# Four moves inside the attention stage of a two-block transformer kernel: VectorE's LRU product, GpSimd's sums and weight requests, and two PSUM reads

## The reference, cut to what matters

```python
def masked_softmax(s, mask):
    s = jnp.where(mask, s.astype(jnp.float32), NEG)
    return jax.nn.softmax(s, axis=-1) * mask
# nsa_mixer: per block of 128 queries, 8 heads, three branches
    p_cmp = masked_softmax(s, dist >= 0)            # over 31 compressed keys
    p = masked_softmax(s, (dist >= 0)[:, :, None])  # selected keys
    p = masked_softmax(s, mask)                     # window keys
    return (g * o).sum(axis=2).reshape(B, S, NSA_WIDTH)
# first_block
    y_a = (y_a * jax.nn.silu(g_nsa)) @ w_proj_a
    y_b = rglru_mixer(u_lru, conv_w, conv_b, lru_wa, lru_ba, lru_wx, lru_bx, lru_lambda)
    y_b = (y_b * jax.nn.silu(g_lru)) @ w_proj_b
    gate_a, gate_b = jnp.split(merge_g, N_BRANCHES, axis=-1)
    m = jax.nn.sigmoid(gate_a) * y_a + jax.nn.sigmoid(gate_b) * y_b
    x = x + m @ w_out
# second_block
    mod = (c @ w_ada[l] + b_ada[l])[:, None, :]
    shift1, scale1, gate1, shift2, scale2, gate2 = jnp.split(mod, 6, axis=-1)
```

## Time and profile before

| what | us |
|---|---|
| median of 3 runs | 1329.16 (1327.74 to 1331.72) |
| the profiled execution, its own time | 1331.02 |
| its span in the trace | 1329.2 |
| PE matmuls busy | 1220.5 (92%) |
| DVE busy | 584.6 (44%) |
| ACT busy | 302.9 (23%) |
| POOL busy | 261.6 (20%) |
| DMA of POOL's queue (q0) | 17.96 MB in 10176 packets |

### The profile page before, as it was taken

One profiled execution on the slowest core, in us unless ns is written; L12 is line 12 of the kernel. 1 busy time (PEld: TensorE's weight loads), 2 busy tenths in 40 slices (PEclk: granted clock), 3 DMA queues, 4 the chain that ended last, 5 costly groups with the idle time before them and its releaser, 6 DMA issues.

```text
span 1329.2 us, 13605 instructions
## 1 busy us (share of the span) xinstructions
PE 1220.5 (92%) x5048; PEld 712.3 (54%) x5048; DVE 584.6 (44%) x1469; ACT 302.9 (23%) x716; POOL 261.6 (20%) x218
## 2 busy tenths in 40 slices
PE   7899998899989999999999899999999799887785
PEld 3455446566744444588874446677654444333232
DVE  3114395588737751208972367422223522321121
ACT  3213643333310000223032255200001211110010
POOL 7200024355400000071600020313200112111100
PEclk9999998899999999999999999999999889988888
DMA  9525110214377612313140202202276589999992
GB/s 326 109 72 127 64 52 12 96 64 143 99 248 255 218 63 101 130 45 127 65 167 23 64 0 65 69 0 64 64 276 266 193 340 402 407 409 402 408 356 83
DMA packets 93255, 215.13 MB, mean 162 GB/s; under 512 B 20297, under 2 KB 51289, under 8 KB 81367
## 3 DMA queue, kind: packets, MB, share of 16 engines
q1 hardware_dynamic: 79664, 193.08, 39.6%
q0 software_dynamic: 10176, 17.96, 5.5%
q10 hardware_dynamic: 3344, 3.16, 0.7%
HBM read 207.79 MB, written 14.75 MB: 167 GB/s over the span
## 4 chain that ended last, share of the span: by engine, by line
PE 69%; SPq 12%; DVE 8%; DMA 5%; ACT 2%; issue 2%; POOL 0%; POOLq 0%; DVEq 0%; ACTq 0%
SPq L2849 11%; PE PS L2363 7%; PE PS L1038 5%; PE PS L1492 4%; PE PS L1570 4%; PE PS L2426 4%; PE PS L1754 4%; PE PS L1756 4%; PE PS L2532 3%; PE PS L612 3%; PE PS L2964 3%; PE PS L1800 2%; PE PS L1501 2%; PE PS L1812 2%; PE PS L682 2%
## 5 line engine op out<-in xcount | busy, mean ns | idle before, releaser
L1332 POOL TENSOR_SCALAR AN<-AN,SM 128x128 f32<-128x128 f32 (+3 forms) x64 | 78.6, 1236 | 198.9 <-DVE SM L1428 198.9
L2964 PE MATMUL PS<-AN,HT 128*64 128x512 f32 x272 | 87.3, 660 | 18.4 <-DMA AN<-in_w_up 8.7
L1355 DVE SCALAR_TENSOR_TENSOR AN<-AN,COLA 128x256 f32<-128x256 f32 x168 | 84.1, 501 | 5.0
L3043 DVE TENSOR_TENSOR HT<-HT,PS 128x256 f32<-128x256 f32 x16 | 6.7, 421 | 152.2 <-ACT HT L3021 152.2
L612 PE MATMUL PS<-W,HT 128*128 128x512 f32 (+1 forms) x192 | 70.5, 528 | 0.0
L2964 PEld LDWEIGHTS PS<-AN,HT 128*64 128x64 f32 x272 | 28.7, 153 | 73.6 <-issue 73.2
L1492 PE MATMUL PS<-HT,W 128*128 128x512 f32 x128 | 58.1, 599 | 0.0
L2532 PE MATMUL PS<-W,AN 128*128 128x512 f32 x128 | 57.6, 597 | 0.0
L1314 ACT ACTIVATE AN<-PS,SM 128x128 f32<-128x128 f32 (+3 forms) x64 | 33.7, 527 | 104.3 <-DVE SM L1405 104.0
L1570 PE MATMUL PS<-W,AN 128*128 128x512 f32 x128 | 55.5, 593 | 1.9 <-DVE GBC L1369 1.9
L2341 POOL TENSOR_TENSOR AN<-W 128x512 f32<-128x512 f32 x8 | 10.1, 1268 | 234.1 <-DMA W<-in_w_in 98.6
(11 more groups left out here) (530 smaller groups left out, 2351.7 us busy)
## 6 DMA issues: line engine op xcount, KB each, us to landing
W<-in_w_in SPq DMA_DIRECT2D x14, 2048.0 KB, 8.9
W<-in_w_down SPq DMA_DIRECT2D x20, 1024.0 KB, 23.0
AN<-in_w_ada SPq DMA_DIRECT2D x17, 1024.0 KB, 5.3
AN<-in_w_gate SPq DMA_DIRECT2D x15, 1024.0 KB, 18.4
AN<-in_w_up SPq DMA_DIRECT2D x15, 1024.0 KB, 29.2
AN<-in_w_down SPq DMA_DIRECT2D x12, 1024.0 KB, 18.9
W<-in_w_gate SPq DMA_DIRECT2D x10, 1024.0 KB, 21.7
W<-in_w_up SPq DMA_DIRECT2D x10, 1024.0 KB, 30.8
```

The source lines that it names most:

```text
L1332: pool.tensor_scalar(PU[u % 5][:, 0:n], PU[u % 5][:, 0:n], RSUM[:, u:u + 1], None, ALU.mult).then_inc(*sc_pool.up(u))
L1355: dve.scalar_tensor_tensor(out=a, in0=wt[:, c, :], scalar=ca["c2"][:, c:c + 1], in1=a, op0=ALU.mult, op1=ALU.add).then_inc(*ada_dve.up(p, c))
L2964: t = pe.matmul(u.ap[r, :].rearrange("p (n f) -> p n f", n=2), XGT[e % 2][:, c, r], w_gu(3 * e + half)[:, c], start=c == 0, stop=c == 7)
```

## The change

Nothing is added or removed; every engine executes the same instructions as before. Four things move.

1. DVE's product with GL (L1232, four instructions) goes from step 33 to step 34.
2. In `pool_attention` the request of a half part of `w_ada` stood ahead of the step's multiply L1332 and now stands behind it. The requests are now L1331 and the multiply L1327.
3. `dve_out` (L1434) goes from the end of its step to the start; `dve_mod` (L1373) goes from the start of the step with r == 3 to behind the scale in the step before.
4. GpSimd's sums of hT go behind two sets of small requests, of `cmp_b` (L773) and of the LRU's weights (L674).

```diff
         if step == 33:
->       if step == 34:
             wd.wait_ge(*lru_act.at("gl"))
             for m in range(4):
                 dve.tensor_tensor(UC[:, m, :], UC[:, m, :], GL[:, m, :], ALU.mult)...
 # pool_attention
         for step in range(NU + 2):
-            p, half = divmod(step - 34, 4)
-            if 0 <= p < ATT_PARTS and half in (0, 2):
-                wg.wait_ge(*(ada_dve.at(p - 1, 3 + 2 * half) if p else lru_dve.at("y", 3)))
-                pool.dma_start(STAGE[0]...).then_inc(*part_in[half // 2].up(p))
             u = step - 2
             if u >= 0:
                 n = (UNITS[u][0] + 1) * 128
                 wg.wait_ge(*sc_dve.at(u // 2, "gate"))
                 wg.wait_ge(*B.use("qk", u).out)
                 pool.tensor_scalar(PU[u % 5][:, 0:n], PU[u % 5][:, 0:n], RSUM[:, u:u + 1], ...)
+            p, half = divmod(step - 34, 4)
+            if 0 <= p < ATT_PARTS and half in (0, 2):
+                wg.wait_ge(*(ada_dve.at(p - 1, 3 + 2 * half) if p else lru_dve.at("y", 3)))
+                pool.dma_start(STAGE[0]...).then_inc(*part_in[half // 2].up(p))
 # dve_attention
             p, r = ada_at(step)
+            if step >= 22 and (step - 22) % 16 == 0:
+                dve_out(dve, wd, (step - 22) // 16)
             if step in FILL and fill_at(step)[2] and fill_at(step)[1] != 1:
                 dve_group(dve, wd, *fill_at(step)[:2])
-            if r == 3 and 0 < p <= ATT_PARTS:
-                dve_mod(dve, wd, p - 1)
 ...
             if step >= 2 and step % 2 == 0 and step <= NU:
                 dve_scale(dve, wd, step // 2 - 1)
+            if r == 2 and 0 < p <= ATT_PARTS:
+                dve_mod(dve, wd, p - 1)
             if step in SUM_AT:
                 dve_group_sum(dve, wd, *SUM_AT[step])
-            if step >= 22 and (step - 22) % 16 == 0:
-                dve_out(dve, wd, (step - 22) // 16)
 # pool_program
-        pool_sums(pool, wg)
         pool_b1(pool, wg)
         pool_bd(pool, wg)
+        pool_sums(pool, wg)
```

More of the change, by code:

```diff
@@ L1228, in dve_lru @@
             dve.tensor_tensor_scan(UC[:, m, :], RG[:, m, :], IG1[:, m, :], 0.0, ALU.mult, ALU.add).then_inc(*lru_dve.up("h", m))
-        if step == 33:
+        if step == 34:
             wd.wait_ge(*lru_act.at("gl"))
@@ L1321, in pool_attention @@
         for step in range(NU + 2):
-            p, half = divmod(step - 34, 4)
-            if 0 <= p < ATT_PARTS and half in (0, 2):
-                wg.wait_ge(*(ada_dve.at(p - 1, 3 + 2 * half) if p else lru_dve.at("y", 3)))
-                pool.dma_start(STAGE[0].rearrange("p (c n) -> p c n", c=8)[:, 2 * half:2 * half + 4],
-                               wada[:, 2 * half:2 * half + 4, 256 * PARTS[p]:256 * PARTS[p] + 256]).then_inc(*part_in[half // 2].up(p))
             u = step - 2
@@ L1332, in pool_attention @@
                 pool.tensor_scalar(PU[u % 5][:, 0:n], PU[u % 5][:, 0:n], RSUM[:, u:u + 1], None, ALU.mult).then_inc(*sc_pool.up(u))
+            p, half = divmod(step - 34, 4)
+            if 0 <= p < ATT_PARTS and half in (0, 2):
+                wg.wait_ge(*(ada_dve.at(p - 1, 3 + 2 * half) if p else lru_dve.at("y", 3)))
+                pool.dma_start(STAGE[0].rearrange("p (c n) -> p c n", c=8)[:, 2 * half:2 * half + 4],
+                               wada[:, 2 * half:2 * half + 4, 256 * PARTS[p]:256 * PARTS[p] + 256]).then_inc(*part_in[half // 2].up(p))
     def ada_sum(p):
```

## The result

The changed kernel takes 1362.09 us in the median of four runs (1357.38 to 1365.89), beside 1330.44 us for the kernel before: a ratio of 1.0238, with a 95% interval of 1.0199 to 1.0277. It is slower by 31.7 us. The forecast was 1344.3 us, with a range up to 1353: the direction was right, and the forecast of 15.1 us slower was about half of what it is. The profiled execution has a span of 1363.7 us and took 1365.89; PE is busy for 1230.9 us of it (90%), before for 1220.5 us with the same 5048 matmuls.

What follows compares the result with a forecast made beforehand. PE, busy 92% of the span, was taken as the bound. The loop's 14.7 us less 1.1 of slack, 13.6, plus 1.5 for the clock gave +15.1: median 1344.3 us, range 1340 to 1350, 8 in 10 within 1335 to 1353.

Steps and rivals of the forecast that it cites:

- The loop: Steps 34 to 62: scale, multiply, request, landing, use, scale form 14 links, together 118.0 us against 101.5 before.
- the landing, 4.0 us for all 14: Each w_ada half-part request in the loop takes 4.0 us from issue to landing, the median in the kernel before.
- rival of longer landings: Landings of 4.5 us in the mean cost 7 us more, half speed at both places 3.2: 1354.5 us; chance 0.08.
- The start of the loop: The scale of step 34 ends at 256.5 us in place of 258.3, 1.8 us earlier.
- The product's gain: PE's wait for L1249 falls from 5.5 to 2.4 us and the half-speed stretch goes: 5.5 us on PE, alone.
- The clock's price: Steps 38/39 and 54/55: longer PE waits for DVE's compressed chain bring half speed; 1.5 us, between 0 and 4.7.
- the 1.1 us of slack: At the stage's end, PE's slack before unit 61's transposes takes up some 1.1 of the loop's 14.7 us.
- The other moves at nothing: dve_out ahead, dve_mod earlier and GpSimd's sums later each taken as 0; dve_out gains at most 0.5 us, dve_mod 1.
- The estimate of 3.2 us a landing: Skill's rule, 2.0 us fixed plus bytes, for 512 KB: links 0.8 us shorter, change costs 3.9 us, 1333 us.
- PE's busy share over the stage: Sign that the forecast is right: PE's busy share over the attention stage is lower by a tenth.

Runs made afterwards that it cites:

- a multiply more: Changed kernel with each w_ada request moved behind the multiplies of both units: 1377.37 us, ratio 1.0364.
- 0.8 us less of landing: Changed kernel with w_proj_a held back and each of the 14 w_ada requests cut to 256 KB: 1341.21 us, ratio 1.0104.
- the held transfer: Changed kernel, with SyncE issuing the 2 MB of w_proj_a only once VectorE has begun the second half of the last w_ada part: 1351.82 us, ratio 1.0148.
- product alone: Kernel before with only VectorE's product with GL moved to step 34: 1324.98 us, ratio 0.9957.

## Why the prediction was half right

**The loop.** Right, and by its own numbers. From the scale of step 34 to that of step 60 the 13 links took 115.1 us (multiply starts 260.17 and 375.25 in the changed kernel), where the sum had 109.4 and the kernel before 94.5 us. Single links match closely: 8.04 for 8.01. The two experiments that change one item, a multiply more and 0.8 us less of landing, moved the 14 links by about 14 times the item. The surplus of 5.7 us sits in four links. From 34 to 36 (1.3 us over the sum) and from 50 to 52 (0.9) the multiply ran beside DVE's L1015 and took 2.15 and 2.54 us in place of 1.37 and 1.68. From 48 to 50 (1.1) the landing of the request at 320.26 took 5.3 us. From 54 to 56 (2.0) DVE waited 4.2 us for a product of PE, which ran at half clock until 351.4.

**The step that failed: the landing, 4.0 us for all 14.** I carried the durations of the kernel before over to requests that start 7 to 28 us later (5.8 of it in that profile the later start of the stage); even my rival of longer landings went no further than 4.5 us in the mean. For the last request the later time was another situation: it came 1.0 us behind two transfers of 1 MB that before began 7.0 us after it. It landed in 14.3 us, and the held transfer gave 10.3 us back. This term of the sum was 4.0 and measured 14.3. With it the forecast would have been 1354.6 us. The SP queue's row of L1447 at 356.17 was in the trace, 3.5 us behind the scale of step 60. In my own sum that scale was due at about 366, so the last request at about 368 and the transfer at about 369, and I did not lay the two side by side. By these figures alone the order of the two was open, and it is the order that decided: 1.2 us ahead of the transfer a request landed in 4.3 us, 1.0 us behind it in 14.3.

**The start of the loop.** The scale of step 34 was forecast 1.8 us earlier than before. Measured from the stage's start it was 4.0 us earlier (103.8 after 107.9). Of the 2.2 us between the two, 1.2 us is a stretch at low clock ahead of step 22 (its eight matmuls of L1038 took 3.62 us at 204.65 in the profile before and 2.92 us in the changed one; nothing that moved stands there, and they took 2.7 to 3.6 us over the other profiles, so this part is chance), and 0.9 us comes in step 23, where PE no longer waits for L1434; the sum had allowed 0 to 0.5 us for that.

**The product's gain.** The wait fell as worked out, 5.5 to 2.4 us. The clock did not stay up: in the changed kernel the window 262 to 266 us reads 0.50. That half of the reason was wrong, though it did not count in the forecast, where the loop takes all of this gain but the earlier scale. The 4.7 us of work at half speed were short as well: before, the clock was at 0.50 until 263.9 us, which is 5.6 us of work.

```profile
262.00:266.00 4.00, 4.00 (x20) 2.83 (x20) 0.00 (x0) 0.95 (x3) 2.35 (x3) 0.50 0.42 134
```

**The clock's price and the stage's end.** The 1.5 us for the clock were right in kind. PE waited 4.2 us for L1373 in step 55 and ran at 0.50 from 347.6 to 351.4; that is the link that was 2.0 us over. It ran at 0.50 once more behind the last landing, from 396 to 403.5, which the forecast lacked. There the 1.1 us of slack that the sum took off were not found: from the scale of step 62 to the merge it was 6.6 us, where 6.1 before less 1.1 is 5.0. The 12.2 us by which PE's matmuls grew over the stage are far more than this; I take it that most of them passed while PE would otherwise have waited for the loop, but no run separates the two.

**The account.** For the stage the sum gave 15.1 us and the profiles 29.0. Of the 13.9 us between them the last landing makes 10.3, the other 13 links 5.7, the end of the stage 1.6 and its start -2.2; the 1.5 us for the clock had a place of their own in the sum and are taken off here, since they are inside the links and the end. The 2.7 us between the stage and the medians of the runs stay open.

**The other moves at nothing.** The sums: confirmed within 0.2%. The bank reads: 1 to 2 us of gain by stage and waits, where the upper bounds were 0.5 and 1 us, and not resolved by the runs.

**The estimate of 3.2 us a landing**, from the Trainium skill, "DMA: Bandwidth & Descriptors", section "Anatomy of one DMA — SWDGE (gpsimd) path". The trace does not agree for 512 KB, counted from the start of the issue to the semaphore: 4.0 us, and the loop keeps that pace. 3.2 us is what half the bytes took.

**The rivals.** Longer landings (chance 0.08) was the nearest, with 1354.5 us, but that is luck: it had all 14 a little longer, and there was one much longer. No rival reaches the 1362.1 us. Of the signs, PE's busy share over the stage fell by 6 points (91% to 85%) and not by ten, since the slower clock stretched its work.

## What to carry to other kernels

When a request is moved behind an instruction that waits, follow what the landing releases: if that leads back to the same wait, the whole round trip becomes a period, and its sum, not the single stall, is the price. When a request starts later, write down what the other queues issue at that new time, since the duration of a landing was measured beside the old neighbours. Of a move in several parts, run each part alone; here one of four cost 35 us and the others together gain 5.

## What the runs showed of the hardware

- From GpSimd a request of 512 KB landed in 4.0 us (median of 14; 4.0 to 4.2 in the other profiles) and one of 256 KB in 3.2 us, so half the bytes save 0.8 us. Single ones of 512 KB took up to 6.2 us, in one kernel 7.4 us, with no w_proj_a transfer near; why is not shown.
- The same 512 KB took 13.3 and 14.3 us when 2 MB from another queue had been issued about 1 us ahead, 10.6 us when they had been issued 4.2 us ahead, 4.1 us when they were held back, and 4.3 us when it was issued 1.2 us ahead of them. In the three slow cases it landed within 0.8 us of the second of the two 1 MB transfers, and the first of these had landed earlier.
- TensorE's granted clock stayed at 1.00 behind one wait of 2.7 us and fell to 0.50 behind one of 2.4 us (product alone: 0.61 in the 3.15 us behind it; changed kernel: 0.50 from 262 to 266). The length of the last wait alone does not tell. PE was busy before both.
